# Compressed-key attention with its norms as factors, and the convolving feed-forward in wide products

## The reference

```python
def conv_ffn(hn, w_up, conv_w, conv_b, w_down):        # first block; F = 2816
    u = causal_dwconv(hn @ w_up, conv_w) + conv_b      # three taps along the tokens
    gate, val = jnp.split(u, 2, axis=-1)
    return (jax.nn.silu(gate) * val) @ w_down

def swiglu(h, w_gate, w_up, w_down):                   # second block, four times
    return (jax.nn.silu(h @ w_gate) * (h @ w_up)) @ w_down

def mla_mixer(h, positions, w_in, q_a_norm, kv_a_norm, w_q_b, w_kv_b, q_norm, k_norm, w_out):
    c_q, c_kv, k_rope = jnp.split(h @ w_in, [384, 640], axis=-1)
    q = rms_norm(c_q, q_a_norm) @ w_q_b                # 8 heads of 128 + 64
    kv = rms_norm(c_kv, kv_a_norm) @ w_kv_b            # 8 heads of 128 + 128
    k = concat([k_nope, broadcast(k_rope)])
    q, k = rms_norm(q, q_norm), rms_norm(k, k_norm)    # over a head's 192
    q, k = rotary on the last 64 of each
    return softmax(causal(q @ k.T * 192 ** -0.5)) @ v @ w_out
```

## Time and profile before

| | |
|---|---|
| three runs | 1743.69, 1746.28, 1746.75 us; median 1746.28 |
| the profiled execution | 1740.71 us, its span 1738.8 us |
| TensorE busy | 1686.6 us, 97% of the span |
| VectorE busy | 1234.3 us, 71% |
| ScalarE busy | 883.9 us, 51% |
| DMA | 165 GB/s mean |
| mean granted TensorE clock | 0.992 of full |

### The profile page before, as it was taken

One profiled execution on the slowest core, in us unless ns is written; L12 is line 12 of the kernel. 1 busy time (PEld: TensorE's weight loads), 2 busy tenths in 40 slices (PEclk: granted clock), 3 DMA queues, 4 the chain that ended last, 5 costly groups with the idle time before them and its releaser, 6 DMA issues.

```text
span 1738.8 us, 32686 instructions
## 1 busy us (share of the span) xinstructions
PE 1686.6 (97%) x13776; PEld 1578.9 (91%) x13776; DVE 1234.3 (71%) x1306; ACT 883.9 (51%) x941; POOL 39.8 (2%) x40
## 2 busy tenths in 40 slices
PE   7999999999999999999999999999999999999997
PEld 7988998999999998999999899998999987999997
DVE  5667768955788878666895766677666776666666
ACT  4376444534443446444675644467444552544446
POOL 0000000100000000000030000000000000000000
PEclk9999999999999999999999999999999997999999
DMA  7524445453445444454542554543555440345541
GB/s 278 184 87 161 160 154 194 147 204 112 176 151 212 155 182 170 170 193 180 196 146 101 179 213 176 190 170 141 200 190 182 162 164 25 113 180 191 184 178 49
DMA packets 42665, 286.93 MB, mean 165 GB/s; under 512 B 4721, under 2 KB 6897, under 8 KB 9169
## 3 DMA queue, kind: packets, MB, share of 16 engines
q1 hardware_dynamic: 38528, 273.70, 43.3%
q0 software_dynamic: 2816, 10.69, 1.7%
q10 hardware_dynamic: 1232, 1.25, 0.2%
HBM read 281.42 MB, written 4.19 MB: 164 GB/s over the span
## 4 chain that ended last, share of the span: by engine, by line
PE 83%; DVE 9%; ACT 4%; issue 3%; DMA 1%; POOL 0%; DVEq 0%; ACTq 0%; POOLq 0%
PE PS L422 82%; DVE arena L1943 2%; DVE ring_lo L1940 2%; ACT ring_hi L1361 2%; ACT arena L1361 1%; DVE arena L1940 1%; DMA arena<-spilled_gates 1%; DVE operand L2003 1%; ACT L1361 1%; DMA ring_raw<-in_w_stream 0%; DVE inv L1997 0%; DMA arena<-in_ple_t 0%; ACT operand L1361 0%; DVE residual L1940 0%; DVE arena L2077 0%
## 5 line engine op out<-in xcount | busy, mean ns | idle before, releaser
L422 PE MATMUL PS<-operand,ring_hi 128*128 128x256 f32 (+1 forms) x4712 | 1108.0, 320 | 23.2 <-DVE operand L2003 14.5
L422 PEld LDWEIGHTS PS<-operand,ring_hi 128*128 128x128 f32 x4712 | 783.3, 191 | 94.6 <-DVE ring_lo L1940 13.4
L422 PE MATMUL PS<-operand,ring_lo 128*128 128x256 f32 x3060 | 862.1, 282 | 1.6 <-issue 1.6
L1940 DVE TENSOR_TENSOR ring_lo<-ring_raw,ring_hi 128x2048 fp32r<-128x2048 f32 x260 | 598.6, 2308 | 181.4 <-ACT ring_hi L1361 181.1
L1361 ACT ACTIVATE ring_hi<-ring_raw 128x2048 fp32r<-128x2048 f32 x260 | 494.4, 1907 | 193.9 <-PE PS L422 188.7
L422 PEld LDWEIGHTS PS<-operand,ring_lo 128*128 128x128 f32 x3060 | 583.7, 191 | 2.1 <-issue 1.8
L422 PE MATMUL PS<-hidden_hi,ring_hi 128*128 128x256 f32 x912 | 258.3, 283 | 1.3 <-DVE hidden_lo L1940 1.3
L422 PE MATMUL PS<-hidden_lo,ring_hi 128*128 128x256 f32 x912 | 258.1, 283 | 0.0
L422 PE MATMUL PS<-hidden_hi,ring_lo 128*128 128x256 f32 x912 | 257.9, 283 | 0.0
L1361 ACT ACTIVATE arena<-PS 128x512 f32<-128x512 f32 (+3 forms) x118 | 75.2, 646 | 290.0 <-PE PS L422 279.9
L422 PEld LDWEIGHTS PS<-hidden_hi,ring_hi 128*128 128x128 f32 x912 | 174.7, 192 | 3.7 <-issue 1.6
(11 more groups left out here) (153 smaller groups left out, 927.3 us busy)
## 6 DMA issues: line engine op xcount, KB each, us to landing
ring_raw<-in_w_stream SPq DMA_DIRECT2D x260, 1024.0 KB, 4.8
spilled_gates<-arena POOLq DMA_DIRECT2D x12, 256.0 KB, 2.6
arena<-spilled_gates POOLq DMA_DIRECT2D x2, 1536.0 KB, 10.1
tables<-in_tables POOLq DMA_DIRECT2D x1, 1344.0 KB, 10.2
residual<-in_x_t ACTq DMA_DIRECT2D x4, 256.0 KB, 6.0
arena<-in_mem_t POOLq DMA_DIRECT2D x1, 1024.0 KB, 17.2
out_t<-residual SPq DMA_DIRECT2D x4, 256.0 KB, 2.1
arena<-in_ple_t POOLq DMA_DIRECT2D x2, 256.0 KB, 4.0
```

The lines of the kernel that those rows point to most:

```text
L422: return nc.tensor.matmul(out, lhs, rhs, start=start, stop=stop, skip_group_check=True)
L1940: return v.tensor_tensor(out, a, b, op)
```

## The change

**Convolving feed-forward.** TensorE's `conv_feed_forward` is gone and `ffn_c` uses `feed_forward`, with wide slabs. ScalarE copies half of each result and now makes the first of the three taps (`first_taps`, Identity with scale and bias); VectorE adds the other half, scales and makes the two later taps. The split of the next up slab moves ahead of the up taps.

**All feed-forwards.** The down banks are cleared by four matmuls of 64 columns instead of eight of 256. In `ffn_1` ScalarE and VectorE do root and reciprocal before the split of the fourth slab (`root_first`).

**Norm sums.** `norm_fold` folds once more, to one tile, and `norm_sum` is one product instead of two (for norms also wanted by token, three instead of six).

**Attention.** The latents' norms are no longer multiplied into queries and keys; they go into the small term that is added before the roots of the head norms (`key_eps`, `query_eps`). Queries are copied, keys multiplied by both gains. Squares are summed by token with single-column products into one bank (`query_sums`, `query_rope_sums`, `key_sums`), placed between the slabs. The key factor is spread over the scores' shape by 16 products with the identity (`spread_keys`) and multiplied into the scores; the query factor is the scale of the exponential. Rotary keys are laid out once for two heads, not for eight. The values come after the scores, and transposes and outputs of the two halves of the heads alternate. The spare products are gone.

```diff
@@ TensorE
-                for k in range(2):
-                    last = mm(bank(b)[:, 0:T], table("ones"), squares[:, k, :], k == 0, k == 1)
+                last = mm(bank(b)[:, 0:T], table("ones"), squares[:, 0, :])
...
-                    for m in range(2):
-                        mm(bank(b)[:, m * T:(m + 1) * T], zeros[:, 0:P], zeros[:], True, False)
+
+                    mm(bank(b)[:, 0:CH], zeros[:, 0:P], zeros[:, 0:CH], True, False)
...
-            conv_feed_forward("ffn_c")
+            feed_forward("ffn_c")
...
+            def spread_keys(e, first):
+                for h in range(4):
                     for tt in range(2):
+                        j = 8 * tt + 4 * e + h
+                        last_ = mm(tiles_of(first, 4)[:, h, tokens(tt)], key_factor[:, j:j + 1].to_broadcast([P, P]),
+                                   table("identity"))
+                last_.then_inc(sem("mla_spread"), 1)
...
+            mla_query(0, 4)
+            pe.wait_ge(sem("output_taken"), taken[0])
+            mla_query(1, 0)
+            pe.wait_ge(sem("latent_squared"), 2)
+            mm(bank(7)[:, 0:T], table("ones"), squares[:, 3, :], True, False)
...
+            last.then_inc(sem("latent_summed"), 1)
+            mla_query(2, 2)
+            pe.wait_ge(sem("mla_squares"), 1)
+            query_sums(range(4), False)
+            operands(2)
+            pe.wait_ge(sem("mla_taken"), 1)
+            mla_keys(0, 4)
+            pe.wait_ge(sem("mla_squares"), 3)
+            query_sums(range(4, 8), True)
+            pe.wait_ge(sem("mla_taken"), 3)
             for n in range(2):
-                last = mm(bank(1 + n), table("swap"), flat(MQ[:, 8:12])[:, 512 * n:512 * (n + 1)])
+                last = mm(bank(2 + n), table("swap"), flat(MQ[:, 8:12])[:, 512 * n:512 * (n + 1)])
             last.then_inc(sem("mla_swapped"), 1)
...
+            mla_keys(1, 0)
+            pe.wait_ge(sem("mla_rope_in"), 2)
+            mm(bank(7)[:, 0:T], table("swap"), kr_gain).then_inc(sem("mla_swapped"), 1)
+            pe.wait_ge(sem("mla_squares"), 4)
+            query_rope_sums()
+            pe.wait_ge(sem("mla_squares"), 5)
+            key_sums(range(4))
+            pe.wait_ge(sem("mla_squares"), 6)
+            key_sums(range(4, 8)).then_inc(sem("mla_sums"), 1)
+            pe.wait_ge(sem("mla_rotated"), 2)
+            mla_scores(7, 4, (0, 1))
+            pe.wait_ge(sem("mla_taken"), 6)
+            spread_keys(0, 2)
+            mla_scores(7, 4, (2, 3)).then_inc(sem("mla_scores"), 1)
+            spread_keys(1, 0)
+            pe.wait_ge(sem("mla_exp"), 1)
+            pe.wait_ge(sem("mla_roots"), 2)
+            mla_scores(6, 2, range(4, 8)).then_inc(sem("mla_scores"), 1)
+            pe.wait_ge(sem("mla_masked"), 1)
+            mla_values(0, 4)
+            pe.wait_ge(sem("mla_exp"), 2)
+            mla_values(1, 0)
+            pe.wait_ge(sem("mla_masked"), 2)
+            pe.wait_ge(sem("mla_probs"), 1)
+            mla_turn(0)
+            pe.wait_ge(sem("mla_probs"), 4)
+            pe.wait_ge(sem("mla_exp"), 5)
+            mla_out(0)
+            pe.wait_ge(sem("mla_probs"), 5)
+            mla_turn(1)
+            pe.wait_ge(sem("mla_probs"), 6)
+            pe.wait_ge(sem("mla_exp"), 6)
+            mla_out(1)
@@ VectorE
                 step(tt_(squares[:, 0:4], squares[:, 0:4], squares[:, 4:8], ALU.add))
-                tt_(squares[:, 0:2], squares[:, 0:2], squares[:, 2:4], ALU.add).then_inc(sem("norm_folded"), 1)
+                step(tt_(squares[:, 0:2], squares[:, 0:2], squares[:, 2:4], ALU.add))
+                tt_(squares[:, 0, :], squares[:, 0, :], squares[:, 1, :], ALU.add).then_inc(sem("norm_folded"), 1)
...
+            def mask_scores(e):
...
+                mul(S0[:, h_], bank(7 - e).rearrange("p (h s) -> p h s", s=P), KS[:, h_, 0:P])
+                step(mul(S1[:, h_], tiles_of(4 - 2 * e, 4), KS[:, h_]))
+                tt_(S0[:, h_], S0[:, h_], per_head("future_penalty"), ALU.add)
+                tt_(S1[:, h_, P:T], S1[:, h_, P:T], per_head("future_penalty"), ALU.add).then_inc(sem("mla_masked"), 1)
...
+            mask_scores(0)
+            mask_scores(1)
+            normed(0)
+            dve.wait_ge(sem("mla_keys"), 2)
+            take_values(0, 4)
+            dve.wait_ge(multiplied, START["mla_kv"] + 2)
+            take_values(1, 0)
+            dve.wait_ge(sem("mla_turned"), 1)
+            v.tensor_copy(flat(PT0[:, 0:4]), bank(2, 2)).then_inc(sem("mla_probs"), 1)
+            normed(1)
+            split_slab(START["mla_kv"] + 3)
```

591 lines of the change are left out of this document (274 added, 317 removed).

## The result

The changed kernel took **1716.12 us** (median, 1715.51 to 1717.25), the kernel before on the same chip 1744.99 (1743.21 to 1746.75): ratio 0.9839, 95% interval [0.9824, 0.9854]. Run again on another chip it was 0.9854 [0.9838, 0.9869]. The forecast was 1714, in a range of 1708 to 1724.

A forecast was written before the change was run, and what follows sets the result against it. TensorE, busy 97% of the span, was taken as the bound. Gains 25.3 + 2.8 + 5.1 = 33.2 us gave 1707.5 from the profiled 1740.7, 1713.1 from the median 1746.3; forecast 1714, range 1708 to 1724.

The forecast's parts named there:

- Attention, 25.3 predicted: Attention, end of `mla_in` to start of `mla_out`: 90.4 us falls to 65.1, a gain of 25.3 us, bounds 8 to 32.
- I price it at nothing in the forecast: Attention: the half clock, 20.4 us long and costing 10.2, goes with the 8-row products; its cause is priced at nothing.
- three waits of the tail: Attention's end: TensorE waits 2.2 us for mask and normalising, 2.2 for VectorE's transpose copy, 1.4 for the second transposes' copy.
- rival E: Attention: 20 new hand-overs between engines each cost 0.5 us more, 10 us in all: 1724; chance 0.10.
- rival A: Attention: sums by token put the clock down for a while, price 1.7 to 10.2 us: 1716 to 1724; chance 0.22.
- `ffn_c`, 2.8 predicted: `ffn_c`: 2.1 + 0.2 + 1.3 - 1.7 + 0.9 = 2.8 us gained from loop, start, end, norm sum and clearing.
- The tail: End of `ffn_c`: last down slab starts 9.0 us after the last up slab instead of 7.23, loss 1.7 us.
- The loop: `ffn_c` loop: a pair goes from 17.28 to 17.07 us, 10 pairs 2.1 us; VectorE's chain of 16.2 stays under it.
- Rival B: `ffn_c` loop: VectorE sets the pace with a chain of 19.2 us, 21 us lost: 1735; chance 0.07.
- Rival C: End of `ffn_c`: the clock falls in the 3.2 us wait, costing 3 us: 1717; chance 0.06.
- Norms and clearing, 5.1 predicted: Outside attention and `ffn_c`: norm sums 3.0, clearing 1.5, `ffn_1`'s new order 0.6, sum 5.1 us.
- Rival D: Attention: one-column sums put the clock down and it stays there, 37 us lost: 1751, slower than before; chance 0.02.

The follow-up runs named there:

- run 10: Changed kernel with the heads' narrow sums of squares left out of attention, three 128-column products instead, factors not the reference's: 1709.29 us, ratio 0.9804.
- runs 3: The changed kernel measured again with no edit: 1718.07 us, ratio 0.9854.
- run 4: Changed kernel with the third slab's rounding and remainder behind the hidden values in each second pair of the `ffn_c` loop: 1723.82 us, ratio 0.9891.
- runs 6: Changed kernel with eight spare 512-column products put among attention's 16 key sums: 1719.87 us, ratio 0.9875.
- run 8: Changed kernel with norm sums as two products (one fold less) and two clearing products a bank, as before: 1719.56 us, ratio 0.9871.
- run 9: Changed kernel with the last two `ffn_c` pairs written out behind four turns, the third slab split late only there: 1715.74 us, ratio 0.9842.
- run 5: Changed kernel with the key rope's swap and the rope's sums ahead of the second half of the keys: 1716.51 us, ratio 0.9854.
- run 1: Kernel before with only the new attention stage: 1727.03 us, ratio 0.9901.
- run 12: Changed kernel with last `ffn_c` pairs written out, `ffn_0`'s first-slab remainder behind the four residual adds, and rope sums ahead of the second key half: 1713.58 us, 0.9833.

## Why the prediction was right, and where not

**The total.** Right: 1716.12 against 1714. The sum of the terms was too large by 8.0 us (33.2 against 25.2 in the profiled executions), and the first pair of profiles hides some of that: by the medians the change was worth 28.9. The profiled execution of before was 4.3 under its median, that of after 0.5 under. So the nearness of the total, 2 us, is in part luck: of the 8 us that attention fell short, 3.7 came back as spread between executions.

**Attention, 25.3 predicted, 17.1 measured: the step that failed** is "I price it at nothing in the forecast" of the half clock's cause. The rest of the ledger held to about 2 us. TensorE was busy 67.73 of the 73.30 us; 15.4 of that lay at half clock (10.2 and 5.17), which is 7.7 us of cost. At full clock the work is 60.0 where the list said 57.9, and the idle time 5.6 where it said 7.2: 65.6 against 65.1. In sum the 8.2 us are 7.7 of clock and 2.1 of work that the list had too low, less 1.6 of idle time. The list of work was short in the kernel before as well: the idle time there is 6.4 (90.38 less 83.98), not 7.7.

The three waits of the tail came out as 1.99, 1.53 and 1.21, against 2.2, 2.2 and 1.4. So the chain was laid correctly (rival E is out), and rival A, which had a chance of 0.22, is what happened in the main: the clock falls for 10.2 us in the key sums and scores, which cost 5.1, within its bounds of 1.7 to 10.2. The other 2.6 of the 7.7 were lost in the turns, behind a wait of 1.99 us. No rival had a fall there, and run 10 has it without the sums; in the runs 3, 4, 6 and 8 it is missing, and why is open. The argument against A, "full-size matmuls follow at once", was wrong in its force: they followed, and the first 4.4 us of them ran at half clock themselves (the first eight score products 4.84 us where they cost 2.6 at full clock).

What should have been read from the trace of before: the stretch at half clock there was taken for a property of 8-row products. The products by token give the array one column to work on. The change swapped one form that fills little of the array for another, so a fall should have been in the forecast and not only among the rivals. (That the 8-row and 8-column products brought the fall before is read from the trace alone; no run parted them.) In all 11 profiled executions with the new attention and its sums, 10.2 to 20.5 us of it ran at half clock, never less.

**`ffn_c`, 2.8 predicted; its stretch gave 3.0, and 4.5 where the clock did not fall.** The tail was right: 9.16 us from the end of the last up slab (622.28) to the last down slab (631.44), 9.0 predicted; the wait in it is 3.25, 3.2 predicted. The loop too: nine pairs in 153.69 us are 17.08 each, predicted 17.07, TensorE without idle time at full clock. VectorE's chain, in the pairs in which it was behind, took 16.36 us (`hidden_lo` at 480.71, 497.07 and so on to 562.52), 16.2 predicted; from there on it waits for TensorE. Rival B is out. Rival C happened, at 1.5 us and not 3, in 5 executions of 7.

The start came out otherwise than laid: from the clearing of the banks to the first down slab it takes 12.48 us before and 12.51 after. The new wait for that slab's split (0.59, 0.9 predicted) stands there and takes all that the narrow clearing and the two slabs ahead of the loop save. The 2.15 us of the old wait are all in the stretch of the table. With them the prediction's steps up to the last hidden product make 2.1 + 2.15 - 1.7, some 2.5; measured are 2.3 without the fall (168.55 against 170.86) and 0.8 with it (170.04).

The other 2.2 us of the stretch lie between the last hidden product and `ffn_0`. By run 8 norm sums and clearing are 0.8 of them. The other 1.4 are the wait ahead of the norm sum that the prediction did not have (run 9). PE in order of time, the kernel before and the changed one:
```profile
642.86 1.02 PE L422 MATMUL PS<-arena,tables 128*128 128x256 f32 x4
645.01 1.99 PE L422 MATMUL PS<-arena,tables 128*128 128x256 f32 x8 [1.13 <-ACT arena L1361]
646.66 0.59 PE L422 MATMUL PS<-operand,ring_hi 128*128 128x256 f32 x2
```
```profile
638.75 2.75 PE L424 MATMUL PS<-arena,tables 128*128 128x256 f32 x12
641.15 0.59 PE L424 MATMUL PS<-operand,ring_hi 128*128 128x256 f32 x2
```
So that 3.0 stands beside 2.8 is luck: 1.4 us that nobody had laid out made good for the 1.5 of the fall.

**Norms and clearing, 5.1 predicted elsewhere, 5.1 measured** by what is left of 25.2. That this agrees to the tenth is luck too: it is a remainder, and up to "c" alone executions differ by 4 us. The better figure is run 8's, 5.3 by place and 0.4 more in attention. The 0.8 of it in "c to 0" lie behind `ffn_c`, at the start of `ffn_0`; in `ffn_c` itself the clearing gained nothing, for the reason above. Run 8 counts the norm sums and the clearing only, without the 0.6 for `ffn_1`'s order. Where they fell was not as listed: 3.6 ahead of `ffn_c`, more than the 3.0 that the list had for all norm sums together, and nothing visible between `ffn_0` and `ffn_2`, since a fall of 3.4 us at half clock behind the 2.7 us wait in front of `ffn_1` took back up to 1.7 there. That wait was 2.72 in the earlier trace rows and is 2.73 now.

**Rival D** needed 33 us of work at half clock; there were 15.4. Its price doesn't follow from its own words: 43.7 us of work at double cost would give 1758, not 1751.

## What to carry to other kernels

Where a profile shows a stretch at half clock over narrow products, a change that only swaps their shape should be priced with that stretch kept, not dropped. Here neither a few wide products among them nor a break in the block saved it (runs 6 and 5). Less narrow work and shorter waits might; no run here tried them alone. Where a change makes a wait of some 3 us, count a fall behind it as a case with a chance of its own: here 3.4 us at half clock, 1.2 to 1.5 us lost, in 5 of 7 executions with a wait of 3.2 us at the end of `ffn_c`, and both times that a wait of this length stood elsewhere (3.21 us in run 4, 3.26 in run 10). And when work leaves a queue's way at one end, look at both ends of the loop and at the next consumer of the same queue: here one moved slab brought a wait of 3.2 us early in the loop in one version, and gave back 1.4 of 1.6 us at the next norm sum in another.

## What the runs showed of the hardware that was not expected

- The clock falls in a stretch in which TensorE has no idle time and does one-, two- and eight-column products: at 1418.75 and 1425.58 in run 5, and it returned between them during 24 wide block matmuls. The Trainium skill, "TensorE: Matmul & The Clock Gate", section "Why this matters for your kernels", names idle gaps over about 3 us between bursts; no gap stood there, so this trace goes beyond it. For the wait at the end of `ffn_c` the traces agree with it roughly: 5 falls behind seven waits of 3.2 us, none behind four of 1.6 to 2.2 us. Elsewhere a long wait was not needed: in the turns of the changed kernel it fell behind one of 1.99 us.
- But it also fell behind the wait of 2.72 us in front of `ffn_1` in all 12 executions of kernels with the rest of the change, and in neither of the two without it, before and run 1. The wait is the same to 0.02 us. The instant is not tied to the wait: the clock fell between 0.8 us ahead of its end (run 12) and 1.4 us behind it (run 8). So two executions without a fall may be chance; what makes the difference is open, and no run was made for it.
- Stretches at half clock had lengths of 3.4, 6.8, 10.2, 13.7 and 20.5 us and nothing between, apart from the last of a program.
- In attention 10 us more at half clock went with about 4 us more of length (136.00 with 10.2, 137.4 to 138.5 with 17.1, 139.0 to 140.2 with 20.5, the run with spare products left out).
- The executions of one kernel differ by up to 9 us (run 12, 1707.98 to 1716.84). The profiled executions of the changed kernel and its variants had between 29 and 46 us at half clock in all; that this makes the spread is likely, but only the profiled executions show their clock.
